# The untaken branch for crowded experts: a loop over 32 experts with a body for one, TensorE's flag load before its last spread, and filler products on both sides of the branch

## What is computed

```python
def hier_moe(x, w_group, w_expert, w_gate, w_up, w_down):
    ...
    g_sel = jnp.argmax(g_prob, axis=-1)
    ...
    top_p, top_i = lax.top_k(jax.nn.softmax(e_logits, axis=-1), MOE_TOP_K)
    ...
        h = jax.nn.silu(xb @ w_gate[e]) * (xb @ w_up[e])
        return h @ w_down[e]
    ...
    out = jax.ops.segment_sum(yb * row_w[:, None], row_tok, num_segments=T + 1)[:T]
```

## Time and profile before

| | us |
|---|---|
| median of 3 runs | 1975.72 |
| lowest and highest run | 1972.38, 1976.1 |
| the profiled execution's own time | 1973.94 |
| its span, first to last instruction | 1972.1 |
| PE busy | 1894.7 (96% of the span) |
| DVE, ACT, POOL busy | 607.1, 432.0, 59.5 |
| PE's mean granted clock, share of full speed | 0.986 |
| 2 MB loads to the ring at their fastest | about 427 GB/s |

### The profile page before, as it was taken

One profiled execution on the slowest core, in us unless ns is written; L12 is line 12 of the kernel. 1 busy time (PEld: TensorE's weight loads), 2 busy tenths in 40 slices (PEclk: granted clock), 3 DMA queues, 4 the chain that ended last, 5 costly groups with the idle time before them and its releaser, 6 DMA issues.

```text
span 1972.1 us, 20850 instructions
## 1 busy us (share of the span) xinstructions
PE 1894.7 (96%) x8531; PEld 1026.5 (52%) x8531; DVE 607.1 (31%) x1502; ACT 432.0 (22%) x953; POOL 59.5 (3%) x60
## 2 busy tenths in 40 slices
PE   8999999999999998999999999999889999899999
PEld 8888654344433433455434443333456556458874
DVE  3666342011111103145201111110435554424752
ACT  2333111010000101142101000100134433206770
POOL 0000000000000000000000000000100000001110
PEclk9999999999999998999999999999999999999999
DMA  9433349999999996224999999999520331231521
GB/s 387 180 145 145 140 162 400 422 428 427 427 428 427 427 424 259 85 115 195 404 423 427 428 427 429 427 428 427 217 93 1 128 128 48 81 128 43 214 99 51
DMA packets 41266, 526.22 MB, mean 267 GB/s; under 512 B 4512, under 2 KB 7104, under 8 KB 9424
## 3 DMA queue, kind: packets, MB, share of 16 engines
q1 hardware_dynamic: 38240, 514.52, 62.8%
q10 hardware_dynamic: 2928, 10.31, 1.4%
HBM read 523.73 MB, written 1.08 MB: 266 GB/s over the span
## 4 chain that ended last, share of the span: by engine, by line
PE 81%; DMA 12%; DVE 3%; ACT 2%; issue 1%; POOL 0%; ACTq 0%; SPq 0%; DVEq 0%
PE ps L195 35%; PE ps L653 17%; DMA ring<-in_wu 9%; PE ps L676 9%; PE ps L685 4%; PE ps L623 3%; DMA ring<-in_wd 3%; PE ps L1138 1%; PE ps L1287 1%; PE ps L1125 1%; PE ps L949 1%; PE ps L471 1%; PE ps L1090 1%; PE ps L618 1%; PE ps L543 1%
## 5 line engine op out<-in xcount | busy, mean ns | idle before, releaser
L653 PE MATMUL ps<-ring,work 128*64 128x512 f32 x2048 | 450.1, 593 | 14.0 <-DMA ring<-in_wu 11.6
L653 PEld LDWEIGHTS ps<-ring,work 128*64 128x64 f32 x2048 | 146.8, 137 | 310.5 <-issue 286.8
L195 PE MATMUL ps<-xT,ring 128*128 128x256 f32 (+3 forms) x1344 | 295.8, 379 | 2.9 <-DMA ring<-in_w_xz 2.0
L195 PEld LDWEIGHTS ps<-xT,ring 128*128 128x128 f32 x1344 | 247.2, 193 | 43.3 <-issue 4.4
L676 PE MATMUL ps<-ring,work 128*64 128x512 f32 x1024 | 227.2, 596 | 3.0 <-ACT work L1496 2.3
L195 PE MATMUL ps<-ring,xT 128*128 128x256 f32 (+2 forms) x672 | 204.5, 462 | 2.6 <-DVE xT L2239 1.9
L195 PE MATMUL ps<-ring,big 128*128 128x512 f32 x448 | 200.2, 604 | 3.5 <-ACT ring L1782 2.4
L2081 DVE TENSOR_TENSOR work<-work,ps 128x512 f32<-128x512 f32 x32 | 22.0, 687 | 530.6 <-PE ps L653 530.6
L195 PEld LDWEIGHTS ps<-ring,xT 128*128 128x128 f32 x672 | 126.3, 191 | 72.8 <-issue 59.9
L676 PEld LDWEIGHTS ps<-ring,work 128*64 128x64 f32 x1024 | 70.6, 137 | 137.1 <-issue 131.4
L195 PEld LDWEIGHTS ps<-ring,big 128*128 128x128 f32 x448 | 85.5, 194 | 107.6 <-issue 104.5
(11 more groups left out here) (365 smaller groups left out, 1599.2 us busy)
## 6 DMA issues: line engine op xcount, KB each, us to landing
ring<-in_wg SPq DMA_DIRECT2D x64, 2048.0 KB, 19.7
ring<-in_wu SPq DMA_DIRECT2D x64, 2048.0 KB, 23.0
ring<-in_wd SPq DMA_DIRECT2D x64, 2048.0 KB, 22.4
ring<-in_w_odd SPq DMA_DIRECT2D x8, 2048.0 KB, 8.4
ring<-in_w_xz SPq DMA_DIRECT2D x7, 2048.0 KB, 17.2
ring<-in_w_qkv SPq DMA_DIRECT2D x6, 2048.0 KB, 15.4
ring<-in_w_bc SPq DMA_DIRECT2D x4, 2048.0 KB, 15.3
ring<-in_ssm_out SPq DMA_DIRECT2D x4, 2048.0 KB, 8.9
```

The lines of the kernel that those rows point to most:

```text
L195: i = e.matmul(bout, lhs(k), rhs(k), start=start and k == ks[0], stop=stop and k == ks[-1])
L653: last = e.matmul(b[64 * j:64 * j + 64, :], x[:, 4 * a + k, 64 * j:64 * j + 64], w[:, 4 * j + k, :], start=a + k == 0, stop=a + k == 4)
```

## The change

Three edits, all in what surrounds the branch:

- `crowded` on PE, ACT and DVE becomes a loop of 32 iterations with the body for one expert. On SP (`sync_crowded`) it stays a loop of 16 with two experts, since its addresses are computed from the pair.
- `tensor_moe` loads PE's flag before the last `tensor_spread` and hands the register to `crowded`, in both layers.
- The 18 filler products behind the branch of layer 0 become 5, and 6 new ones stand before it, between the turning of the meta tokens and the wait for `mzT_in`.

```diff
                 tensor_down(e, l, p)
+            v = e.value_load(flag(l))
             tensor_spread(e, l, NE // 2 - 1)
             if l == 0:
                 e.wait_ge(*mz_in(0))
...
                 last.then_inc(*z_mm.up(0, 2, 0))
+                tensor_warm(e, row_b[0], 6)
                 e.wait_ge(*mzT_in(0))
             e.wait_ge(*moe_res(l))
-            crowded(e, l, tensor_crowded, x_pe, X_PE, x_go_pe)
+            crowded(e, l, tensor_crowded, x_pe, X_PE, x_go_pe, v)
...
-        def crowded(e, l, body, own, keys, go):
-
-            v = e.value_load(flags[:, l:l + 1][0:1, 0:1].bitcast(I32))
+        def flag(l):
+            return flags[:, l:l + 1][0:1, 0:1].bitcast(I32)
+
+        def crowded(e, l, body, own, keys, go, v=None):
+
+
+            v = e.value_load(flag(l)) if v is None else v
+            paired = body is sync_crowded
             with e.If(v):
-                with e.Fori(0, NE // 2) as i:
-                    for j in range(2):
+                with e.Fori(0, NE // 2 if paired else NE) as i:
+                    for j in range(2 if paired else 1):
                         body(e, l, i, j)
...
         def tensor_attention(e):
             for t in range(2):
                 if t == 0:
-                    tensor_warm(e, row_b[0], 18)
+                    tensor_warm(e, row_b[0], 5)
```

## The result

| us | before | after |
|---|---|---|
| median, both kernels run in turn on one chip | 1972.38 (7 runs) | 1964.89 (7 runs) |
| lowest and highest run | 1968.15, 1976.1 | 1963.58, 1968.89 |
| the profiled execution's own time | 1973.94 | 1963.7 |

The ratio after to before is 0.9963, with a 95% interval of 0.9948 to 0.9979: 7.3 us less, between 4.1 and 10.3. The change makes the kernel faster by over 0.2%, and the time lies in the predicted range, 3.4 us under the predicted value.

The account below looks back on a forecast made before the run. PE, busy for 96% of the span, was taken to bound the kernel. Gains of 9.2 and 1.2 us less two clock losses of 2.4 gave 5.6 us off 1973.94: 1968.3 us, range 1963.5 to 1972.5.

Parts of the forecast that it names:

- The stall is a fetch and the short body removes it: PE's branch in both layers: jumps past the running and next packet wait, 6794 and 4865 ns; one-expert bodies end that.
- Rival A: PE's branch, both layers: the stall stays despite the shorter jump; 4.3 us gained in all, 1969.6 us, chance 0.14.
- The branch then costs 0.07 us, as DVE's: PE's branch in both layers: without the stall it takes what DVE's does, 0.07 us.
- Projection of tile 0 at 756.0: Layer 0 behind the branch: the first projection starts at 756.0 instead of 765.22, a gain of 9.2 us.
- Fillers and load at nothing: Around PE's branch: five fillers behind, six ahead and the moved flag load add nothing to the path.
- Weights come in time: Layer 0's projection: none of the weight loads is late; the first landed near 745, needed at 756.0.
- The clock takes back 2.4 us in layer 0: Layer 0's first projection: PE's clock falls to half in the wait, losing 2.4 us, bounds 0 and 3.4.
- rival B: Both layers behind the branch: the clock holds, 10.4 us gained, 1963.5 us, chance 0.12.
- Layer 1: 1.2 us gained, 2.4 lost: Layer 1's projection: starts 1.2 us earlier, behind DVE, but at half clock, losing 2.4 us; ends 1.2 us worse.
- Rivals C and D: C: too few fillers, layer 0 at half clock, 1986.5 us, chance 0.03; D: weight load swallows its gain, 1975.1, chance 0.07.
- The sum: Both layers together: 9.2 - 2.4 + 1.2 - 2.4 = 5.6 us off 1973.94, giving 1968.3 us.

Follow-up runs that it names:

- e2: Kernel after with two-expert bodies again, so the moved load and changed fillers alone; 1966.91 us, ratio to before 0.9972.
- e3: Kernel after with 80 never-run filler products in front of PE's loop inside the branch, a jump of about 376; 1972.52 us, one execution.
- e4: Kernel after with 55 never-run filler products in front of PE's loop inside the branch, a jump of about 326; 1963.37 us, one execution.
- e9: Kernel after with PE's flag load back behind the last spread; 1959.99 us, one execution.
- e5: Kernel after with 18 fillers instead of 5 behind the branch of layer 0; 1960.32 us, ratio to before 0.9938.
- e6: Kernel after with 20 fillers in layer 1 between the meta tokens' projection and the turning of tile 0; 1959.57 us, ratio to before 0.9936.
- e11: The kernel of e4 again (55 never-run fillers against the kernel after), timed over 12 executions; 1965.68 us, ratio to before 0.9979.
- e7: Kernel after with 18 fillers behind layer 0's branch and 20 in layer 1's wait; 1958.63 us, ratio to before 0.9928.
- e10: The kernel of e3 again (80 never-run fillers against the kernel after), timed over 7 executions; 1963.91 us, ratio to before 0.9966.

## Why the prediction was right

- **The stall is a fetch and the short body removes it.** Right: 350 and 322 ns with the short body, a stall again with the long one (e2), and put back in one layer at a time by e3 and e4; in all eight stalls a packet lands 1.3 to 1.5 us before the branch ends. What PE holds stands in no view: that it is the packet it runs and the next is my reading of the places, and by the count e2's layer 1 (482) doesn't fit it. The packets fell from 72 to 70, as forecast. Rival A falls: PE's short jump doesn't stall. The packet was sized a little short: the 17,894 records leave out 540 others of PE, 534 of them on semaphores, and with them it is (17,894 + 540) / 72 = 256 to a packet and not 249, an estimate that puts all 72 packets down to PE. By 2 x 256 = 512 the kernel before still stalls in both layers, in layer 1 by a small margin (522 by the count above).
- **The branch then costs 0.07 us, as DVE's.** This step failed: 0.32 to 0.35 us in the kernel after, five times DVE's; why is open. It cost nothing, because PE waits 2.13 us for DVE behind it in layer 0, and 1.59 and 4.80 us in layer 1.
- **Projection of tile 0 at 756.0, that is 6.96 us behind `moe_res`.** Measured 6.82. The forecast of a 9.2 us gain became 9.35.
- **Fillers and load at nothing.** Right on the path: the fillers ended at 751.04, 2.1 us ahead of tile 0, and e9 has the same P1. But "their cost is nothing either way" missed that enough of them are worth something: e5 and e6 keep the clock with 18 and 20, for 0.28 us of P1 and for nothing.
- **Weights come in time.** Right: in the chain the projection follows ACT's copy, not a load.
- **The clock takes back 2.4 us in layer 0.** It fell and came back as forecast (0.50 from 755.2 to 758.2, 1.00 behind it), and the size was too large here: 1.55 us in the profiled execution, and 1.7 on the mean of five kernels (8.68, 9.97, 9.03, 9.41 and 7.13 us for the projection, against 7.13), one of which lost nothing. So rival B's case turns up in layer 0 in a single execution. Where PE had waited for DVE, the clock was at half behind 4.80 us in layer 1 of the kernel after (0.50 from 1389.8 to 1396.5) and, with five fillers, behind 2.13 us in layer 0 (0.50 from 755.2 to 758.2; e4, e6 and e11 too, 0.50 for at least 6.6 us each); behind the 1.58 us of e9 it held.
- **Layer 1: 1.2 us gained, 2.4 lost.** Measured 1.33 and 2.29: the stall removed here was worth nothing or less, as forecast. B never turned up here: all seven kernels without this stall and without e6's fillers took 11.3 to 12.6 us for tile 0 and not 9.73.
- **Rivals C and D** fall: the clock came back after 3 us, and the stretch between the layers took 617.0 us, not longer than the 617.9 of before, with no more idle time of PE in it (15.2 us, before 17.1).
- **The sum.** Forecast 5.6 us in the places, measured 6.9; the term that was off is layer 0's clock (0.85 of the 1.3). The predicted time came out 3.4 us high, and two errors of one sign make that up: it was set against one execution of 1973.94, while the median of before in the comparison was 1972.38, so the base was 1.6 us high; and the gain was forecast at 5.6 us where the medians show 7.5. The time alone would not have told the forecast from its rival: 1964.89 lies nearer to B's 1963.5 than to 1968.3. It is the places, half clock in both layers, that speak for the forecast.

## What to carry to other kernels

Code that never runs can cost time: on PE a jump over it was cheap (0.32 to 0.41 us, not 4.9 to 6.8) only where by my count it landed no further than the next instruction packet. So keep a skipped body well under 250 records (my estimate of a packet; with one of 208, none of 14 branches stalled), or move it out of the way (not tried here), and look for a branch that takes microseconds on one engine and nanoseconds on the others. When a stall goes, ask at once who is late next and what the engine's clock does in the wait that opens there. Fillers that were a waste behind a stall are worth having in a wait on another engine (e7: 18 and 20 small products brought P2 forward by 1.3 and 2.3 us). How many are enough isn't known from here: five gained nothing that could be shown.

## What the runs showed of the hardware

- PE's branch where it doesn't stall takes 0.32 to 0.35 us, 0.41 in layer 1 of e3 and e10; DVE's takes 0.06 to 0.07, ACT's and SP's 0.05.
- A branch of PE whose target lay 330 to 493 records from the last packet's arrival took 0.32 to 0.41 us, in 18 of 18 (hits). One at 482 to 593 took 4.9 to 6.8 us, in eight of eight (misses), all with the data transfers at 0.93 to 1.01 of their full share; with an idle DMA system none was measured. By the places above every hit lands in the packet behind the one that runs, so none shows what a jump inside one packet costs.
- Two edits that each help didn't add where they removed the same wait (8.5 and 4.1 us alone, 9.35 together). And the stall removed in front of a wait on another engine gained nothing (layer 1: P2 at 23.30 before and 24.25 after).
- The moments at which the clock falls and comes back differ at the same program: behind stalls of 6.4 and 5.9 us at one branch the first projection took 9.44 us in e3 (0.50 from 753.6 to 767.1) and 7.13 in e10 (0.50 from 751.0 to 757.7, 1.00 behind it). An untouched stretch of 615 us took 612.8 to 617.9 us; between before and e6, 5.0 of the 5.2 us are PE's longer busy time at a mean clock of 0.99 against 1.00.
